# One kernel of two transformer blocks: the first mixer's work beside its first gemm, and unread products in waits

## The reference, cut to what matters

```python
mod = (silu(c) @ ada_w[layer] + ada_b[layer])   # six parts: sh1, sc1, g1, sh2, sc2, g2
h = rms_norm(x, norm1_g) * (1 + sc1) + sh1
rq, rk, rv, rg, aq, ak, av = split(h @ w_in)    # 7 x 512 columns
rq, rk = rotary(rq), rotary(rk) * 128 ** -0.5
ret = head_rms(retention(rq, rk, rv)) * silu(rg)            # 4 heads of 128
att = chunk_attention(rms_norm(aq), rms_norm(ak), av, bias) # 8 heads of 64
x = x + g1 * (concat(ret, att) @ w_out)
x = x + g2 * grouped_moe(rms_norm(x, norm2_g) * (1 + sc2) + sh2)
```

## Time and profile before

| what | value |
|---|---|
| median of three timed runs | 2419.2 us |
| the profiled execution | 2429.3 us, its span 2427.5 us |
| PE busy | 2271.5 us (94%) |
| DVE busy, ACT busy | 1480.0 us (61%), 1077.3 us (44%) |
| mean granted PE clock | 0.957 of full |
| DMA | 477.79 MB, mean 197 GB/s |

### The profile page before, as it was taken

One profiled execution on the slowest core, in us unless ns is written; L12 is line 12 of the kernel. 1 busy time (PEld: TensorE's weight loads), 2 busy tenths in 40 slices (PEclk: granted clock), 3 DMA queues, 4 the chain that ended last, 5 costly groups with the idle time before them and its releaser, 6 DMA issues.

```text
span 2427.5 us, 36226 instructions
## 1 busy us (share of the span) xinstructions
PE 2271.5 (94%) x15742; PEld 1977.9 (81%) x15742; DVE 1480.0 (61%) x1422; ACT 1077.3 (44%) x1123; POOL 74.3 (3%) x128
## 2 busy tenths in 40 slices
PE   6998799898989889999999999898999999999999
PEld 4667699776778779877779998787999899877998
DVE  5664688867863565689865554545555555534554
ACT  3314433456754533477653345334433534435332
POOL 2003011000000000000000000000000000020000
PEclk9987899999999989999999999798999999989999
DMA  8941599879944074599955543003555455432553
GB/s 321 360 183 36 194 331 327 290 252 324 394 159 139 20 243 156 192 358 364 350 166 190 190 160 118 1 4 122 175 190 190 162 195 189 159 92 83 192 180 119
DMA packets 261118, 477.79 MB, mean 197 GB/s; under 512 B 8464, under 2 KB 150896, under 8 KB 257632
## 3 DMA queue, kind: packets, MB, share of 16 engines
q1 hardware_dynamic: 251264, 431.81, 51.3%
q0 software_dynamic: 9696, 43.66, 5.3%
HBM read 473.30 MB, written 2.14 MB: 196 GB/s over the span
## 4 chain that ended last, share of the span: by engine, by line
PE 80%; DVE 8%; ACT 5%; DMA 4%; issue 2%; POOL 0%; DVEq 0%; ACTq 0%; SPq 0%; POOLq 0%
PE psum L945 7%; PE psum L947 7%; PE psum L946 7%; PE psum L962 3%; PE psum L963 3%; PE psum L964 3%; PE psum L916 3%; PE psum L917 3%; PE psum L918 3%; DVE w_lo L2439 3%; PE psum L1295 2%; PE psum L1297 2%; PE psum L1296 2%; PE psum L1212 2%; PE psum L1214 2%
## 5 line engine op out<-in xcount | busy, mean ns | idle before, releaser
L2439 DVE TENSOR_TENSOR w_lo<-ring,w_hi 128x2048 fp32r<-128x2048 f32 x320 | 731.2, 2290 | 454.5 <-ACT w_hi L1881 450.3
L1881 ACT ACTIVATE w_hi<-ring 128x2048 fp32r<-128x2048 f32 x320 | 611.6, 1914 | 565.9 <-PE psum L947 143.7
L945 PE MATMUL psum<-h_hi,w_hi 128*128 128x256 f32 x1408 | 398.9, 283 | 1.6 <-DVE h_lo L3047 1.3
L947 PE MATMUL psum<-h_hi,w_lo 128*128 128x256 f32 x1408 | 398.4, 283 | 0.0
L946 PE MATMUL psum<-h_lo,w_hi 128*128 128x256 f32 x1408 | 398.4, 283 | 0.0
L945 PEld LDWEIGHTS psum<-h_hi,w_hi 128*128 128x128 f32 x1408 | 270.1, 192 | 3.6 <-issue 1.7
L946 PEld LDWEIGHTS psum<-h_lo,w_hi 128*128 128x128 f32 x1408 | 270.1, 192 | 1.4
L947 PEld LDWEIGHTS psum<-h_hi,w_lo 128*128 128x128 f32 x1408 | 270.1, 192 | 0.0
L2439 DVE TENSOR_TENSOR w_lo<-pool,w_hi 128x2048 fp32r<-128x2048 f32 x65 | 148.9, 2290 | 51.6 <-ACT w_hi L1881 51.0
L1295 PE MATMUL psum<-w_hi,h_hi 128*128 128x512 f32 x384 | 156.3, 407 | 15.3 <-DVE w_lo L2439 8.5
L1881 ACT ACTIVATE w_hi<-pool 128x2048 fp32r<-128x2048 f32 x65 | 124.6, 1918 | 68.2 <-PE psum L1297 17.6
(11 more groups left out here) (450 smaller groups left out, 4013.3 us busy)
## 6 DMA issues: line engine op xcount, KB each, us to landing
ring<-in_exp_w_down SPq DMA_DIRECT2D x48, 1024.0 KB, 7.3
ring<-in_exp_w_gate SPq DMA_DIRECT2D x47, 1024.0 KB, 7.2
ring<-in_ffn_pre_w_in SPq DMA_DIRECT2D x44, 1024.0 KB, 5.1
ring<-in_ffn_post_w_in SPq DMA_DIRECT2D x44, 1024.0 KB, 5.1
ring<-in_exp_w_up SPq DMA_DIRECT2D x32, 1024.0 KB, 6.9
pool<-in_exp_w_up SPq DMA_DIRECT2D x32, 1024.0 KB, 7.9
ring<-in_ada_w SPq DMA_DIRECT2D x24, 1024.0 KB, 5.2
pool<-in_ada_w POOLq DMA_DIRECT2D x32, 768.0 KB, 6.2
```

The source lines that it names most:

```text
L945: pe.matmul(o, wh[:, k, fs], h_hi[:, k, :], start=k == 0, stop=False)
L947: m = pe.matmul(o, wl[:, k, fs], h_hi[:, k, :], start=False, stop=k == KD - 1)
L1881: act.activation(w_hi[:, (s["split"] + r) % 3, :], piece(s["pieces"][r]), ACT.Copy)\
L2439: dve.tensor_tensor(w_lo[:, slot, :], piece(s["pieces"][r]), w_hi[:, slot, :].bitcast(F32), ALU.subtract).then_inc(sem("w_lo"), 1)
```

## The change

- `even_in` computes its chunks in the order rq, rk, aq, ak, rv, av, rg (`EVEN_ORDER`). ACT alone copies each chunk, both banks at once, and the last through Silu.
- The modulation pieces are placed anew (`EVEN_ADA`): none between the first two weight pieces and none behind the eighth and ninth; third 1 comes first, and five pieces come behind the gemm, four of them inside the attention on DVE.
- Rotation, the turning of rq, rk, aq and ak, the retention and the norm of aq and ak lie between the pieces of `even_in`. The norm of the retention is scaled in the attention. All four heads' scores have a bank of their own.
- The biases of the gate rows are added by DVE to one row of the accumulator (`bias_row`), not by PE. The first gate row is summed behind the gemm, the second in the router; the columns of sh2 and sc2 and the memory keys' norm and turning go beside `even_out`.
- The attention's bias loads start as soon as the memory products and the rotation are done. PE waits for the biases job by job.
- `warm` products: the 24 behind retention and norms go, 6 stand before the attention; new ones stand in both routers, in three waits of the RWKV preparation, in both memory attentions, at the tails of all attentions, and before `even_out` and `b_out`. They leave the output as it is.

The core of the diff:

```diff
-    p.gemm("even_in", EVEN_W, between=[(row, third) for row in range(KD) for third in (1, 2)])
+EVEN_ORDER = [0, 1, 4, 5, 2, 6, 3]
+EVEN_ADA = [None] + [(row, 1) for row in range(6)] + [None, None, (6, 1), (7, 1), (0, 2), (1, 2), (2, 2), (3, 2)]\
+    + [(row, 2) for row in range(4, 8)]
+    p.gemm("even_in", EVEN_W, between=EVEN_ADA)
...
POOL:
-            pl.wait_ge(sem("w_used"), PL.done_at[PL.gemms["even_in"]["base"] + 6])
-            pl.wait_ge(sem("mod_rows"), 1)
+            pl.wait_ge(sem("mem_ps"), 2)
+            pl.wait_ge(sem("rotated"), 1)
...
PE:
+            def beside_even(n):          # after piece n of 14
+                second_memory(n)
+                if n in (9, 11):
+                    for e in moved("even_in", 2 if n == 9 else 3):
+                        pe.wait_ge(sem(e[0]), e[1])
+                    pe.wait_ge(sem("rotated"), 1)
+                    even_turned("ret_qk", (0, 1) if n == 9 else (2, 3))
+                if n in (10, 12):
+                    pe.wait_ge(sem("tr_act"), n // 2 - 4)
+                    pe.wait_ge(sem("tr_dve"), n // 2 - 4)
+                if n == 12:
...                                       # scores of four heads
+                if n == 13:
...                                       # wait for decays, values of four heads
+                    pe.wait_ge(sem("heads_ok"), 1)
+                    even_turned("att_qk", range(4))
+            def beside_out(n):
+                if n == 2:
+                    transposes("mem_k0", ("heads_ok", 2))
+                    transposes("mem_k1")
+                if n == 3:
...
+                    modulation((2, 3))
...
-            (the steps from the memory keys to warm(6, 0), one behind the other)
+            gemm("even_in", beside_even)
+            transposed("att_qk")
+            pe.wait_ge(sem("ada_used"), KD + 8)
+            gate_row(0, 6)
+            pe.wait_ge(sem("ret_moved"), 2)
+            warm(6, 4)
+            for e in moved("even_in", 6):
                 pe.wait_ge(sem(e[0]), e[1])
+            attention("att")
...
router:
+                if layer == 0:
+                    pe.wait_ge(sem("mod_moved"), 2)
+                    gate_row(1, 0)
+                warm(9 if layer else 4, 2)
                 pe.wait_ge(sem("group_picked"), layer + 1)
...
+                warm(5, 2)
                 pe.wait_ge(sem("comb_tok"), layer + 1)
...
+                warm(3 if layer else 7, 2)
attention, before the values' and the turning's waits:
+                        if kind in ("mem0", "mem1") or j >= len(jobs):
+                            warm(2 if j == 2 else 1, 6 + j % 2)
+                        if kind in ("mem0", "mem1"):
+                            warm(3 if j == 1 else 1, 4 + (j - 1) % 2)
RWKV preparation: warm(4, ...) before shift_mixed, warm(6, 2) before rw_sig, warm(4, 2) behind the turned queries
ACT, ahead of chunk c's copy (and behind the split of piece 2c+3):
+                if c == 3:
+                    act.wait_ge(sem("ada_used"), KD + 7)
+                if c == 4:
+                    even_turned("ret_qk", (0, 1))
+                if c == 5:
+                    heads(0)
+                    even_turned("ret_qk", (2, 3))
+                if c == 6:
...                                       # retention's copies, squares, att_qk, heads(1)
DVE:
+            def even_first(c):            # ahead of the splits of pieces 2c+3 and 2c+4
+                if c == 2:
+                    bias_row(0, KD + 6)
...
+                    rotate(0)
+                if c == 3:
+                    rotate(1)
+                if c == 5:
+                    heads_stats(0, qk, 64)
+                if c == 6:
+                    heads_scale(0, qk, 64, [(8, 16, 1, 0.125)])
...
+            def beside_att(j):
+                if j == 1:
+                    heads_scale(1, rr, P, [])
+                if j == 2:
...                                       # retention times silu(rg)
+                if 3 <= j <= 6:
+                    ada_piece(ADA_PIECES - 7 + j)
```

More of the change, by code:

```diff
@@ L1413, in _ @@
             gemm("a_in")
+            for e in moved("a_in", 3):
+                pe.wait_ge(sem(e[0]), e[1])
+            warm(4, pair_of("a_in", 3))
             pe.wait_ge(sem("shift_mixed"), SHIFT_TILES)
@@ L1808, in norm, with gemm @@
                                        scale=NGAIN[nm][:, k:k + 1]).then_inc(sem("h_split_hi"), 1)
-            def gemm(nm, last=None):
+            def gemm(nm, last=None, first=None, after=None):
                 g = PL.gemms[nm]
@@ L1817, in gemm @@
                     kind, dst = gemm_dst(nm, c)
+                    if first and kind != "whole":
+                        first(c)
                     if 2 * c + 3 < count:
@@ L1821, in gemm @@
                         last()
+                    if first and kind == "whole":
+                        first(c)
                     if not kind.startswith("resid"):
@@ L1824, in gemm @@
                     ps = bank(pair_of(nm, c))
+                    if kind == "whole":
+                        act.activation(dst, psum[:, pair_of(nm, c):pair_of(nm, c) + 2, :], ACT.Silu if c == 6 else ACT.Copy)\
+                           .then_inc(sem("ev_act"), 1)
+                        if after:
+                            after(c)
                     if nm == "kv" and c == 2:
@@ L1863, in transposes, with even_turned @@
                                        ACT.Copy).then_inc(sem("tr_act"), 1)
+            def even_turned(nm, some):
+                for i in some:
+                    B = TR_BASE[nm] + i
+                    act.wait_ge(sem("tr_done"), B + 1)
+                    act.activation(TRS[nm][i][1], bank(EVEN_BANKS[nm][i]), ACT.Copy)\
+                       .then_inc(sem("tr_dve" if B % 2 else "tr_act"), 1)
             def heads_squares(n, parts):
@@ L1981, in _ @@
+            gemm("even_in", None, even_first, even_after)
+            attention("att", beside_att)
             split_piece("even_out", 0, 0)
@@ L2307, in norm, with gemm @@
                     m.then_inc(sem("h_split_lo"), 1)
-            def gemm(nm, then=None):
+            def gemm(nm, then=None, first=None):
                 g = PL.gemms[nm]
@@ new lines, in rotate, with bias_row @@
+                step(dve.tensor_tensor(x2, x2, co, ALU.mult))
+                dve.tensor_tensor(x1, x1, r1, ALU.subtract)
+                step(dve.tensor_tensor(x2, x2, r2, ALU.add))
+            def bias_row(j, n):
+                row = acc_0[1][0:1, 0:D] if j == 0 else acc_0[2][0:1, D:2 * D]
+                dve.wait_ge(sem("ada_b_in"), 16 + 16 * j)
+                dve.wait_ge(sem("ada_used"), n)
+                step(dve.tensor_tensor(row, row, ada_rows[j], ALU.add))
+            qk = [proj_e[:, t, 2048:3072].rearrange("p (h d) -> p h d", h=16) for t in range(NT)]
@@ L2609, in router @@
+            dve.wait_ge(sem("mem_out"), 64)
             def router(layer):
```

341 lines of the change are left out of this document (181 added, 160 removed).

## The result

The changed kernel takes 2384.9 us (median of four runs, 2383.3 to 2389.3) against 2420.9 us for the kernel before on the same chip (four runs, 2419.0 to 2426.9): ratio 0.985, 95% interval 0.9827 to 0.9873. It is faster by 36 us or 1.5%, and the forecast of 2356 us with its range down from 2378 missed it. The profiled execution of after took 2385.7 us, close to its median; that of before had taken 2429.3, which is 8 us above its own.

What follows compares the result with a forecast made beforehand. The prediction took TensorE as the bound, with time to win where it waits or runs at half clock. Terms -47.7 + 1 + 6 - 3.2 - 19 = -62.9 took 2419.2 to 2356 us, range 2338 to 2378.

Steps and rivals of the forecast that it cites:

- Part 5: Even attention: DVE's added work costs time, the first jobs no longer run at half clock; +1 us, bounds -4 and +9.
- Part 6: Second gemm: transposes, column sums and a wait for the memory keys' norm are added where TensorE is full; +6 us.
- Part 7: Unread products elsewhere keep TensorE's clock up: -3.2 us in the expert layers, -19 us in later layers.
- Rival (a): Unread products outside the even mixer don't hold the clock: -22.2 shrinks to about -2, 2376 us; chance 0.17.
- Part 1: Front of the first gemm: earlier weight pieces remove a 4.84 us stall and half-clock products behind it; -7.4 us.
- Part 3: First gemm's end: the last weight piece lands late beside the bias loads and TensorE waits; +6 us, bounds 0 and 15.
- Rival (c): The weight ring starves at the first gemm's end: 15 to 16 us instead of 6, 2366 us; chance 0.15.
- Part 4: Between first gemm and attention: one gate row, 1.7 us, and six unread products, 2.6 us, remain; 4.3 us.
- (b): Even attention: DVE bounds it, modulation pieces delay maxima and the clock falls; +8 us, 2364 us; chance 0.15.
- (d): First gemm: transposes and waits between the pieces cost it full clock; slower by 76 us, 2432 us; chance 0.02.
- (e): First gemm: moved work waits in TensorE's order, nothing gained; each of five waits would cost 12 us; chance 0.01.
- Rival (f): Beside the bias additions DVE and GpSimd shut each other out: decays come 6 us later, 2362 us; chance 0.05.

Runs made afterwards that it cites:

- no six: The changed kernel with the bias loads held back and without the six unread products before the even attention: 2371.4 us, ratio 0.9785 to the kernel before.
- late biases: The changed kernel with the 16 bias loads held back until the first gemm's last weight piece has landed: 2381.6 us, ratio 0.9817 to the kernel before.

## Why the prediction was wrong

The sum was -62.9 us; the two timed comparisons of after gave -36 and -39. In stage means of the traces it is -41. Part by part, each mean over the traces of the table that have or lack the part:

| step | predicted | measured | against |
|---|---|---|---|
| Parts 1 to 4, gemm's first product to the attention's | -47.7 | -43.4 | three of before, five of after |
| Part 5, attention | +1 | +2.3 | the same |
| Part 6, second gemm | +6 | +7.4 | the same |
| Part 7, routers | -3.2 | 0 | seven without, seven with |
| Part 7, RWKV layer | -8 | -6.3 | four without, nine with |
| Part 7, dilated stage | -11 | -1.5 | seven without, seven with |

Part 7 was forecast at -22.2 and measured at -7.8; that is 14 of the 21 us by which the sum missed the stage means. Set against the changed kernels without the fillers alone, both expert layers together gain 0.7 us, the dilated stage 1.3 and the RWKV layer 8.6 (one trace), which leaves the picture as it is.

**The step that failed most is Part 7's dilated term** ("10 us go, less 1"). The mechanism, products in waits hold the clock, acted on something that two other executions of before don't have. The 10 us belonged to that execution and not to the median one, and a sign of it stood in the front matter: the profiled run was 8 to 10 us over the median. I subtracted a difference made on that run from a median that did not contain it. The RWKV term, read from the same trace by the same reasoning, was right in kind and near in size, since that low clock is in every execution. Rival (a) said "the fillers don't hold the clock"; what happened is that there was mostly nothing to hold. The rule of the Trainium skill ("TensorE: Matmul & The Clock Gate", "Part 4: PE-mode transpose") that transposes don't count as activity is neither shown nor refuted: with the fillers the RWKV window had 0.92 in the first trace of after, 0.79 in the second and in that of "no six", and 1.00 in none of nine.

**Part 7's routers** failed at the step from the clock to the time: 0.70 became 0.95 over the first 34 us, on records of which nearly all that came in addition were the fillers, and the layer wasn't clearly shorter. That the weight transfers set its pace is argued, not tested. The share of 0.80 to 1.10 in the earlier trace rows pointed to a layer that waits for transfers, and the prediction allowed for that only in its first weight.

**Part 1** was right about the stall and about 6.7 of 7.4 us (the start of the fourth piece after that of the first, 20.5 us for 27.2 in the first two traces). What was late next isn't DVE, as I wrote, but the ring: ACT waits for its pieces, and TensorE stands once more before the fifth piece, 0.6 to 2.1 us. Rows of after, timelines of ACT and PE:

```profile
81.65 1.91 ACT L1962 ACTIVATE w_hi<-ring 128x2048 fp32r<-128x2048 f32 x1 [7.49 <-DMA ring<-in_even_w_in]
...
85.94 0.50 PE L946 MATMUL psum<-w_hi,h_hi 128*128 128x512 f32 x1 [2.06 <-DVE w_lo L2557]
```

**Part 3** had the right mechanism, place and releaser. Its +6 was some 2 us short: the wait is 4.0 to 6.7 us in five traces, the four heads behind it at half clock cost 2.5 more (1.28 us each for 0.65), and holding the loads back returned 6.4. Rival (c), with 15 to 16 us, is too high.

**Part 4**: the gate row takes 1.7 us and the six products 2.6, exactly as counted; the second is waste. **Part 5** counted on 5 to 6 us of half clock in the attention of before, and that too was in one execution only: against 27.4 us the attention is 3 us longer, against the first trace 0.6 (the first of after: 30.7). Its sum was wrong as well: its own terms, 5 and 2 us for DVE and 1.2 for the bias row less 5 to 6 for the clock, make 2.2 to 3.2 and not 1. That the modulation pieces cost time on the path is confirmed, with 4 us. **Part 6** is right but for the clock: 32 records of one-column sums take 4.49 us instead of 3.6, and the products behind them run at half clock:

```profile
222.75 4.49 PE L1078 MATMUL psum<-keep,pool 128*128 128x1 f32 x32
227.10 0.77 PE L946 MATMUL psum<-w_hi,h_hi 128*128 128x512 f32 x1
227.68 0.63 PE L947 MATMUL psum<-w_hi,h_lo 128*128 128x512 f32 x1
```

Rivals (b), (d) and (e) did not come: the attention's clock is 0.94 and 4 of the pieces' 9.4 us lie on the path, and the first gemm has its full clock to 131.5. Rival (f) is below. (The forecast's own range, -3 and +4 for three terms, would be 2347 to 2368 and not 2346 to 2366.) The range would have held the result if the -22.2 of Part 7 had been bounded by what the other executions show; its bound above, 0 for everything that a single trace shows at half clock, gives 2378, and rival (c) on top of it 2388.

What stays open: what decides in one execution whether the clock falls in the dilated attention, the even attention or the odd mixer. No run here tells that; only that it varies and that fillers narrow it in the dilated stage.

## What to carry to other kernels

Before a half-clock stretch is counted as a gain, compare the profiled run's own time with the median of the timed ones: an excess may be that very stretch, and a second profile settles it. Products in a wait are worth most where the low clock is in every execution; elsewhere they at best steadied a stage here, and ahead of the expert layers (DMA share 0.87 in the first) no gain was clear. When small loads of another queue start beside the last piece of a weight ring, let them wait for that piece to land, and ask of every reordering which engine is next in line for the same transfer.

## What the runs showed of the hardware

VectorE and GpSimd hold each other up: what starts second ends late by up to the whole operation of the other. Timelines of DVE and POOL in after, where the bias additions lie beside the norm's scales, then with late biases, where they don't:

```profile
151.48 14.00 POOL L764 TENSOR_TENSOR pool<-pool 128x128 f32<-128x128 f32 x16 [9.74 <-DMA pool<-in_c_anti]
...
151.71 1.47 DVE L2513 TENSOR_TENSOR pool<-pool,tiny 128x1024 f32<-128x1024 f32 x1
153.22 1.10 DVE L2518 SCALAR_TENSOR_TENSOR pool<-pool,gains 128x512 f32<-128x512 f32 x1
```
```profile
157.35 8.84 POOL L766 TENSOR_TENSOR pool<-pool 128x128 f32<-128x128 f32 x16 [8.46 <-DMA pool<-in_c_anti]
...
145.27 1.22 DVE L2515 TENSOR_TENSOR pool<-pool,tiny 128x1024 f32<-128x1024 f32 x1
146.52 0.69 DVE L2520 SCALAR_TENSOR_TENSOR pool<-pool,gains 128x512 f32<-128x512 f32 x1
```

Sixteen additions take 14.00 us beside DVE and 8.84 without; an operation of DVE over 1024 elements 1.47 and 1.22 us, one over 512 elements 1.10 and 0.69. One by one the additions show how. Rows of POOL, two in after, then the same two sizes with late biases:

```profile
152.07 1.70 POOL L764 TENSOR_TENSOR pool<-pool 128x256 f32<-128x256 f32 x1
158.95 2.51 POOL L764 TENSOR_TENSOR pool<-pool 128x128 f32<-128x128 f32 x1
```
```profile
157.78 0.73 POOL L766 TENSOR_TENSOR pool<-pool 128x256 f32<-128x256 f32 x1
157.35 0.45 POOL L766 TENSOR_TENSOR pool<-pool 128x128 f32<-128x128 f32 x1 [8.46 <-DMA pool<-in_c_anti]
```

The first starts inside the operation of DVE from 151.71 to 153.18 and ends 0.58 us behind it; the second starts inside a modulation product of DVE (158.76, 2.38 us) and ends 0.3 us behind it, with 2.1 of its 2.51 us a wait. The Trainium skill (SBUF - State Buffer, "SBUF: two separate sides") speaks of an exclusive lock in which the loser fully blocks, and these rows agree. Four operations of DVE lose 1.2 us together, 0.15 to 0.42 each, which is at most one addition's own time. So rival (f) had the right mechanism and, with 6 us, too large a size: it took eight operations, and for each the 0.82 us that an addition lasts with its waits in it, where alone it takes 0.45 or 0.73. "The rows speak for the small number" (Part 3) was right about DVE's loss; GpSimd's, 5.2 us over the sixteen, was hidden.

TensorE can lose its clock without standing still. With late biases this window of the RWKV preparation is full, and among its products are 24 records of two columns; 12 records of unread products ahead of them take 2.75 us, 8 behind them 3.62, twice as long each (the window, then TensorE's timeline):

```profile
1472.90:1482.90 10.00, 10.00 (x47) 8.85 (x46) 2.14 (x6) 4.73 (x11) 0.00 (x0) 0.74 0.01 3
```
```profile
1472.20 2.75 PE L1012 MATMUL psum<-gains,keep 128*128 128x256 f32 x12
...
1477.66 5.23 PE L1519 MATMUL psum<-keep,pool 128*128 128x2 f32 x24
...
1483.64 3.62 PE L1012 MATMUL psum<-gains,keep 128*128 128x256 f32 x8
```

A busy share of 1 in a window is no sign that the clock held in it.
